# Encoder layer with expert routing: the second merge pass, the last token tile and the first expert body rearranged

## The reference, cut to what matters

```python
h  = rms_norm(x) * (1 + sc1) + sh1
qa, ka, va, qb, kb, vb, ga, gb = split(h @ w_in)
oa, ob = attention(...) @ w_branch_a, window_attention(...) @ w_branch_b
merged = sigmoid(ga) * oa + sigmoid(gb) * ob
x  = x + gt1 * (merged @ w_out)
h2 = rms_norm(x) * (1 + sc2) + sh2
aff = softmax(h2 @ w_router)            # each group routed by itself
g, idx = top_k(aff.T, cap)              # 128 (sample) or 32 (prompt) rows per expert
hid = silu(h2[idx] @ w_e_gate) * (h2[idx] @ w_e_up)
x  = x + gt2 * scatter_add(idx, (hid @ w_e_down) * g)
y  = rms_norm(x)
```

## Time and profile before

| | us |
|---|---|
| median of 3 runs | 2537.7 (2537.65 to 2543.83) |
| the profiled execution, its device time | 2540.18 |
| its span in the trace | 2538.4 |
| PE busy | 2341.3 (92%) |
| DVE busy | 1673.3 (66%) |
| ACT busy | 1214.5 (48%) |
| POOL busy | 1145.7 (45%) |

### The profile page before, as it was taken

The page is one execution under the profiler, slowest core; times in us unless marked ns, Lnnn a source line. Parts: engine busy times, 40 slices in busy tenths (PEclk is TensorE's granted clock), DMA queues, the critical chain, the costliest instruction groups (busy, mean ns, idle before and its releaser), DMA issues.

```text
span 2538.4 us, 54391 instructions
## 1 busy us (share of the span) xinstructions
PE 2341.3 (92%) x23617; PEld 1698.3 (67%) x23724; DVE 1673.3 (66%) x2040; ACT 1214.5 (48%) x1520; POOL 1145.7 (45%) x713
## 2 busy tenths in 40 slices
PE   8599899998999998587899999999999999999993
PEld 3244577655444456456788888888888888888871
DVE  1855466556222466474888878887788878888862
ACT  2322555466111234143655565666555555666552
POOL 0300111122333323254666766785677666776640
PEclk9799899999999999797999999999999999999997
DMA  8010300311212255154989999999999999999965
GB/s 321 14 34 1 117 1 2 133 68 30 80 50 50 81 160 158 50 188 166 325 302 333 325 323 317 328 322 338 319 317 330 336 314 314 341 327 323 318 230 188
DMA packets 255461, 524.86 MB, mean 207 GB/s; under 512 B 8587, under 2 KB 60924, under 8 KB 255100
## 3 DMA queue, kind: packets, MB, share of 16 engines
q1 hardware_dynamic: 244668, 489.95, 55.3%
q0 software_dynamic: 10560, 31.46, 4.4%
HBM read 493.08 MB, written 28.31 MB: 205 GB/s over the span
## 4 chain that ended last, share of the span: by engine, by line
PE 82%; DVE 10%; ACT 3%; DMA 2%; issue 2%; SPq 1%; POOL 0%; DVEq 0%; ACTq 0%; POOLq 0%
PE ps L1579 22%; PE ps L1580 21%; PE ps L1578 21%; PE ps L1920 4%; PE ps L1730 4%; PE ps L1718 4%; PE ps L1699 2%; DVE arena L1181 2%; DVE arena L1373 1%; DVE arena L1251 1%; PE ps L1709 1%; ACT arena L1032 1%; DMA arena<-w_ada 1%; PE ps L1612 1%; DMA arena<-w_e_up 1%
## 5 line engine op out<-in xcount | busy, mean ns | idle before, releaser
L1579 PE MATMUL ps<-arena 128*128 128x160 bf16 (+2 forms) x5556 | 1394.8, 269 | 28.1 <-POOL arena L751 13.6
L1580 PE MATMUL ps<-arena 128*128 128x160 bf16 (+2 forms) x5555 | 1393.9, 269 | 0.2
L1578 PE MATMUL ps<-arena 128*128 128x160 bf16 (+2 forms) x5462 | 1360.0, 267 | 17.4 <-DVE arena L1510 7.7
L1474 DVE TENSOR_TENSOR arena<-arena 128x2048 bf16<-128x2048 f32 x376 | 922.5, 2458 | 185.6 <-ACT arena L895 185.0
L895 ACT ACTIVATE arena<-arena 128x2048 bf16<-128x2048 f32 x384 | 727.1, 1905 | 230.8 <-PE ps L1580 177.6
L1578 PEld LDWEIGHTS ps<-arena 128*128 128x128 bf16 x5560 | 547.5, 98 | 196.5 <-issue 41.9
L1580 PEld LDWEIGHTS ps<-arena 128*128 128x128 bf16 x5560 | 547.4, 98 | 155.6 <-issue 3.3
L1579 PEld LDWEIGHTS ps<-arena 128*128 128x128 bf16 x5560 | 547.4, 98 | 145.3 <-issue 3.0
L820 POOL TENSOR_TENSOR arena<-arena 128x320 bf16<-128x320 f32 x128 | 285.7, 2232 | 10.0
L817 POOL TENSOR_TENSOR arena<-arena,ones 128x320 bf16<-128x320 f32 x128 | 178.3, 1393 | 175.2 <-DVE arena L1510 174.9
L1118 ACT ACTIVATE arena<-ps 128x160 f32<-128x160 f32 x256 | 77.8, 304 | 321.6 <-PE ps L1580 321.5
(11 more groups left out here) (221 smaller groups left out, 2321.5 us busy)
## 6 DMA issues: line engine op xcount, KB each, us to landing
arena<-w_e_gate SPq DMA_DIRECT2D x64, 2048.0 KB, 9.0
arena<-w_e_up SPq DMA_DIRECT2D x64, 2048.0 KB, 9.4
arena<-w_e_down SPq DMA_DIRECT2D x64, 2048.0 KB, 8.1
arena<-w_ada SPq DMA_DIRECT2D x12, 2048.0 KB, 8.6
arena<-w_in SPq DMA_DIRECT2D x32, 512.0 KB, 5.3
arena<-x_sample SPq DMA_DIRECT2D x16, 512.0 KB, 3.5
arena<-w_in SPq DMA_DIRECT2D x3, 2048.0 KB, 16.3
arena<-w_branch_a SPq DMA_DIRECT2D x32, 128.0 KB, 4.3
```

Source lines behind the costliest of these rows:

```text
L1474: ve.tensor_tensor(lo, stage_half(kind, a), hi, ALU.subtract).then_inc(lo_done, 1)
L1578: pe.matmul(out, w_hi, x_hi, start=start, stop=False)
L1579: pe.matmul(out, w_hi, x_lo, start=False, stop=False)
L1580: return pe.matmul(out, w_lo, x_hi, start=False, stop=stop)
```

## The change

In the second pass `GT` is cut in two: a new step `GD` n is DVE's writing of the diagonals, and `GT` n keeps the product and the copy. `GD` n stands one half block ahead of `GT` n. Block order is rotated by one: `second(k)` maps block k of the second pass to output block k - 1 (mod 8), so that its block 0 is block 7 and uses the split weights that `WS` 7 left behind. `WS` 8 and its load are gone; `WS` 9 moves from after `XO` 3 to after `XO` 2. `RT` and `AT` of the last sample tiles move back by a half block, and one of the top-k rounds moves from block 1 to block 6.

The last token tile's `XO` works in two halves of 512 columns, the first after two of the four `OL` pieces; the square root's table is loaded ahead of it. ACT does half of this tile's `X2`. In all `RT`, ACT instead of DVE scales the softmax. `XS` moves behind the last `X2`, and POOL's split of its result behind the last tile's DMAs.

In the first body the split of weight halves becomes one a step: halves 8 to 15 at f = 0 to 7, and halves 0 to 7 of expert 1 at f = 8 to 15. Its fourth quarter takes the places of its first. At the end, the last `down` waits for a quarter's hidden values at a time.

```diff
@@ -183,7 +183,8 @@
-            s += [("GT", n) for n in range(2)]
+            for n in range(2):
+                s += [("GD", n), ("GT", n)]
@@ -191,11 +192,12 @@
-        if p in (1, 3):
-            s.append(("WS", KD + p // 2))
+        if p == 2:
+            s.append(("WS", KD + 1))
-    tail = {(0, 1): [("X2", ns - 1), ("RT", ns - 2), ("AT", ns - 3)], (1, 0): [("RT", ns - 1), ("AT", ns - 2)],
-            (1, 1): [("AT", ns - 1)], (2, 0): [("GT", 2)], (2, 1): [("GT", 3)], (3, 0): [("GT", 4)], (3, 1): [("GT", 5)], (4, 0): [("GT", 6)], (4, 1): [("GT", 7)]}
+    tail = {(0, 1): [("X2", ns - 1)], (1, 0): [("RT", ns - 2), ("AT", ns - 3)], (1, 1): [("RT", ns - 1), ("AT", ns - 2)],
+            (2, 0): [("AT", ns - 1), ("GD", 2)], (2, 1): [("GT", 2), ("GD", 3)], (3, 0): [("GT", 3), ("GD", 4)],
+            (3, 1): [("GT", 4), ("GD", 5)], (4, 0): [("GT", 5), ("GD", 6)], (4, 1): [("GT", 6), ("GD", 7)], (5, 0): [("GT", 7)]}
@@ -203,13 +205,14 @@
-        for _ in range((0, 1, 2, 3, 3, 3, 2, 2)[m]):
+        for _ in range((0, 0, 2, 3, 3, 3, 3, 2)[m]):
-    s += [("FH", 0), ("FH", 1), ("FL", 0), ("O", ns), ("KM",), ("IS",), ("FH", 2), ("FH", 3), ("FL", 1), ("FL", 2), ("XO", ns), ("FL", 3), ("OL", 0), ("OL", 1), ("X2", ns),
-          ("OL", 2), ("RT", ns), ("OL", 3), ("XS",), ("XO", ns + 1), ("AT", ns), ("FH", 4), ("FH", 5), ("X2", ns + 1),
-          ("RT", ns + 1), ("AT", ns + 1), ("FL", 4), ("FH", 6), ("FH", 7), ("FL", 5), ("K", 0), ("I",)]
+    s += [("FH", 0), ("FH", 1), ("FL", 0), ("O", ns), ("KM",), ("IS",), ("FH", 2), ("FH", 3), ("FL", 1), ("FL", 2), ("XO", ns),
+          ("FL", 3), ("OL", 0), ("OL", 1), ("X2", ns), ("OL", 2), ("RT", ns), ("OL", 3), ("AT", ns), ("XO", ns + 1),
+          ("X2", ns + 1), ("XS",), ("FH", 4), ("RT", ns + 1), ("AT", ns + 1), ("FL", 4), ("FH", 5), ("FH", 6), ("FH", 7),
+          ("FL", 5), ("K", 0), ("I",)]
@@ -332,7 +335,7 @@
-        split = [(3 + n) * CH for n in range(6)]
+        split = [(3 + n) * CH for n in (4, 2, 0, 1, 5, 3)]
@@ -460,11 +464,15 @@
-            return ((5, 3), (4, 2), (0, 1), (3, 4))[q][kind]
+            return ((4, 5), (0, 1), (2, 3), (4, 5))[q][kind]
+        def second(k):
+            return (k - 1) % KD
@@ -480,11 +488,7 @@
-                if s < 4:
-                    return []
-                if s < 12:
-                    return [(0, s + 4)]
-                return [(2, 2 * (s - 12)), (2, 2 * (s - 12) + 1)]
+                return [(0, s + AHEAD) if s < AHEAD else (2, s - AHEAD)]
@@ -633,23 +637,22 @@
-            mw_load(KD)
+            mw_load(KD + 2)
-                if p in (1, 5):
-                    k = p // 4
-                    sp.wait_ge(ws_done, 2 * KD + k + 1)
-                    sp.wait_ge(ws_rest, k + 1)
-                    mw_load(KD + k + 2)
+                if p == 4:
+                    sp.wait_ge(ws_done, 2 * KD + 1)
+                    sp.wait_ge(ws_rest, 1)
+                    mw_load(KD + 3)
-                sp.wait_ge(ws_done, 2 * KD + k - 1)
-                sp.wait_ge(ws_rest, k - 1)
+                sp.wait_ge(ws_done, 2 * KD + k - 2)
+                sp.wait_ge(ws_rest, k - 2)
-            sp.wait_ge(ws_done, 3 * KD)
-            sp.wait_ge(ws_rest, KD)
+            sp.wait_ge(ws_done, 3 * KD - 1)
+            sp.wait_ge(ws_rest, KD - 1)
@@ -756,14 +759,15 @@
-                    gp.tensor_tensor(dst[:, s[1], a:a + w], tmp, ones[:, 0:1].to_broadcast([P, w]), ALU.mult).then_inc(mhigh, 1)
+                    m = s[1] if k == "M" else second(s[1])
+                    gp.tensor_tensor(dst[:, m, a:a + w], tmp, ones[:, 0:1].to_broadcast([P, w]), ALU.mult).then_inc(mhigh, 1)
-                    gp.tensor_tensor(dst[:, KD + s[1], a:a + w], tmp, dst[:, s[1], a:a + w], ALU.subtract)\
+                    gp.tensor_tensor(dst[:, KD + m, a:a + w], tmp, dst[:, m, a:a + w], ALU.subtract)\
-                    gp.wait_ge(ws_hi, 2 * m + 1)
+                    gp.wait_ge(ws_hi, 2 * m - 1)
@@ -784,7 +788,7 @@
-                if k == "XS":
+                if k == "XO" and s[1] == NT - 1:
@@ -1084,24 +1088,45 @@
-                    ac.wait_ge(x1_ready, t + 1)
+                    if t < NT - 1:
+                        ac.wait_ge(x1_ready, t + 1)
-                    ac.activation(xn2[:, t % 2], x1[:, t % 2], ACT.Square, accum_out=rs[:, t % 2, 0:1]).then_inc(ssq, 1)
+                    if t < NT - 1:
+                        ac.activation(xn2[:, t % 2], x1[:, t % 2], ACT.Square, accum_out=rs[:, t % 2, 0:1]).then_inc(ssq, 1)
+                    else:
+                        ac.activation(spare[:, 3:4], ones[:, 0:1], ACT.Sqrt)
+                        for h in range(2):
+                            z = slice(512 * h, 512 * h + 512)
+                            ac.wait_ge(x1_half, h + 1)
+                            ac.activation(xn2[:, t % 2, z], x1[:, t % 2, z], ACT.Square, accum_out=rs[:, t % 2, 4 * h:4 * h + 1])\
+                                .then_inc(ssq, 1)
+                if k == "X2" and s[1] == NT - 1:
+                    b, free = job(s, 1)
+                    for q in range(4):
+                        ins = ac.activation(h2T[1][:, 4 + q, :], b[:, q * P:(q + 1) * P], ACT.Identity,
+                                            scale=A2[:, 4 + q, 0:1], bias=modT[:, 28 + q, 0:1])
+                    ins.then_inc(free, 1)
+                    ac.wait_ge(rt_rec, t + 1)
+                    ac.activation(af[:, t % 2], lg[:, t % 2], ACT.Copy, scale=rst[:, t % 2, 2:3]).then_inc(aff_ready, 1)
+                            if h == AHEAD:
+                                for b in range(2):
+                                    ac.wait_ge(x1_out[b], 8 * NT)
+                                    ac.wait_ge(xn2_out[b], 8 * NT)
@@ -1172,9 +1197,9 @@
-            def modulate(s, dst, A, sh, g):
-                for half in range(2):
+            def modulate(s, dst, A, sh, g, halves=(0, 1)):
+                for half in halves:
@@ -1379,10 +1404,10 @@
-                if k == "GT":
+                if k == "GD":
-                    if n % 4 >= 2:
+                    if n >= 2:
@@ -1408,26 +1433,37 @@
-                    ve.wait_ge(out_done, t + 1)
+                    if t < NT - 1:
+                        ve.wait_ge(out_done, t + 1)
-                    o = ps[:, 2 * (t % 2):2 * (t % 2) + 2].rearrange("p a b -> p (a b)")
-                    ve.tensor_tensor(x1[:, t % 2], o, gt1b[g], ALU.mult).then_inc(out_free, 1)
-                    ve.wait_ge(out_free, t + 1)
-                    ve.tensor_tensor(x1[:, t % 2], x1[:, t % 2], xo[:, t % 2], ALU.add).then_inc(x1_ready, 1)
-                    norm_in(NT + t)
+                    if t < NT - 1:
+                        o = ps[:, 2 * (t % 2):2 * (t % 2) + 2].rearrange("p a b -> p (a b)")
+                        ve.tensor_tensor(x1[:, t % 2], o, gt1b[g], ALU.mult).then_inc(out_free, 1)
+                        ve.wait_ge(out_free, t + 1)
+                        ve.tensor_tensor(x1[:, t % 2], x1[:, t % 2], xo[:, t % 2], ALU.add).then_inc(x1_ready, 1)
+                        norm_in(NT + t)
+                    else:
+                        for h in range(2):
+                            z = slice(512 * h, 512 * h + 512)
+                            ve.wait_ge(*((half_done, 1), (out_done, NT))[h])
+                            ve.tensor_tensor(x1[:, t % 2, z], ps[:, 2 * (t % 2) + h], gt1b[g][:, z], ALU.mult).then_inc(last_mul, 1)
+                            ve.wait_ge(last_mul, h + 1)
+                            ve.tensor_tensor(x1[:, t % 2, z], x1[:, t % 2, z], xo[:, t % 2, z], ALU.add).then_inc(x1_half, 1)
+                        ve.wait_ge(ssq, 2 * NT + 1)
+                        link(ve.tensor_tensor(rs[:, t % 2, 0:1], rs[:, t % 2, 0:1], rs[:, t % 2, 4:5], ALU.add))
+                        norm_in(NT + t)
-                    modulate(s, lambda kk: h2T[t % 2][:, kk, :], A2, 24, group_of(tile_at(t)))
+                    modulate(s, lambda kk: h2T[t % 2][:, kk, :], A2, 24, group_of(tile_at(t)), (0,) if t == NT - 1 else (0, 1))
-                    link(ve.reciprocal(rst[:, t % 2, 2:3], rst[:, t % 2, 1:2]))
-                    ve.tensor_scalar(af[:, t % 2], lg[:, t % 2], rst[:, t % 2, 2:3], None, ALU.mult).then_inc(aff_ready, 1)
+                    ve.reciprocal(rst[:, t % 2, 2:3], rst[:, t % 2, 1:2]).then_inc(rt_rec, 1)
@@ -1784,8 +1820,9 @@
-                        pe.wait_ge(ws_done, 2 * KD + m + 1)
-                        pe.wait_ge(ws_rest, m + 1)
+                        if m:
+                            pe.wait_ge(ws_done, 2 * KD + m)
+                            pe.wait_ge(ws_rest, m)
@@ -1816,15 +1853,16 @@
-                    for k0, k1 in ((0, KD - 1), (KD - 1, KD)):
-                        if p == NT - PT_TILES and k1 == KD:
+                    order = list(range(KD)) if p < NT - PT_TILES else [second(n) for n in range(KD)]
+                    for part in (order[:-1], order[-1:]):
+                        if p == NT - PT_TILES and len(part) == 1:
```

(10 more changed lines are left out.)

9 lines of the change are left out of this document (5 added, 4 removed).

## The result

| | us |
|---|---|
| before, median (4 runs) | 2537.7 (2536.8 to 2543.8) |
| after, median (4 runs) | 2503.9 (2502.6 to 2504.5) |
| after / before | 0.9861, 95% interval 0.9844 to 0.9878 |
| profiled execution: before, after | 2540.18, 2503.61 (spans 2538.4, 2501.8) |
| forecast | 2503.7 (2493 to 2519) |

What follows compares the result with a forecast made beforehand. PE was taken as the bound from 1233.73 us on, and ahead of that its waits, mostly for the diagonals. Terms −1.7 − 25.1 − 0.9 − 6.3 = −34.0 turn the median 2537.7 into 2503.7 us, range 2493 to 2519.

Steps and rivals of the forecast that it cites:

- Projection stage: Before the second pass: PE's 1.73 us wait before an `X2`, for DVE's scaling, should go: −1.7 us (0 to −1.8).
- Second pass: Up to `IS`: waits 18.9 instead of 37.7 us, cold matmuls 6.4 instead of 12.7: −25.1 us (−30 to −20).
- The walk along both lists: Second pass: PE's and DVE's work followed from before block 0, giving remaining waits of 18.9 us.
- the third per us waited: Second pass: cold matmuls cost 0.34 us for each us waited, so 6.4 instead of 12.7 us.
- `IS` to the first body: Stage of 51.53 us: last `X2` at 23.3 instead of 25.9, most given back: −0.9 us (0 to −3).
- First body: Body of 68.36 us: one split a step ends DVE's late products, next body starts at 62.1: −6.3 us (−10 to 0).
- The turn of 15.7 us: First body, slowest buffer: load 9.04, high part 1.91, two low parts of 2.46 us, some 15.7 in all.
- End: Last down product: the 5.04 us wait stays, since PE stands until DVE empties expert 14's products: 0.
- A: Second pass: DVE's low parts run unhindered by POOL's, 1.22 instead of 4.25 us: −12 more, 2492; A or like gain 0.12.
- B: First body turns on the loads: three turns cost 7 us more each, 21 in all: 2525; chance 0.15.
- C: Second pass: DVE keeps its backlog, long waits shrink only 2 or 3 us each, some −20: 2509; chance 0.08.
- D: Second pass: PE stays cold at 1.2 GHz from block 2 on: +44.3 us, 2548 in all; chance 0.04.

Runs made afterwards that it cites:

- e3: The changed kernel with the first body's weight halves split as before (8 to 15 at f = 4 to 11, then two per f): 2512.6 us.
- e5: The changed kernel with the gate load issued just ahead of the prompt's gather held until that gather has landed: 2502.6 us.
- f1: The changed kernel with `XS` and the last high and low parts back in their old places, the last tile still in halves: 2499.5 us.
- e9: The changed kernel with the last down product waiting for all hidden values at once, as before: 2505.6 us (one run).
- e2: The kernel before with only the diagonals (`GD`) written a half block ahead: 2511.4 us, ratio 0.9901.
- e4: The changed kernel with POOL's low part of each second-pass block waiting until DVE has written its own: 2492.0 us.
- e1: The changed kernel with the diagonals `GD` n written again directly ahead of `GT` n's product: 2536.2 us, ratio to the kernel before 0.9999.
- e6: The changed kernel with the split of the next weights (`WS`) ahead of `GT` and `GD` of the same half block, on all engines: 2506.8 us.

## Why the prediction was right, and where it wasn't

The time, 2503.9 after 2503.7, is nearer than its steps. From profile to profile the gain was 36.6, not 34.0; the profiled execution of before lay 2.5 above its median and that of after 0.3 below, so the medians moved by 33.8. Against the forecast the steps below are off by +0.6, −2.4, +3.2, −2.3 and −2.4, and the stretch ahead of them was 0.9 longer. That they come to some 2.5 us only, and that the medians took even this back, is luck; that most of the gain lies in the second pass isn't.

- *Projection stage*, −1.7: it was −1.1. The wait of 1.73 went, but one of 0.91 came at an earlier `X2`, behind the place where `WS` 9 now stands.
- *Second pass*, −25.1: −27.5. The walk along both lists named the waits: 4.4 at the last router step (4.7), 0.5, 4.6 and 6.2 for the diagonals (0.2, 4.5, 6.5), none at the others. That the last agrees to 0.3 is partly luck: in e3, e5, f1 and e9, whose second pass is the same program, it was 4.9, and the pass took 108.4 all the same, with more of it in cold matmuls (PE busy 93.06 in e3, 91.84 here). Of the wait at `IS`, 3.0, only 0.7 came: PE ended its `O` 0.8 us later and DVE its joining a good 1 us earlier than in the walk.

  The cold matmuls cost what the forecast gave them, PE was busy 6.3 us less, but the third per us waited isn't a constant: 6.4 us stood beside 16.6 of waits here (0.38), and by the same 85.5 us of warm work e2 has 7.8 beside 15.8 and e4 3.9 beside 8.4, nearly half. So the price came out because the waits were 2.3 shorter than forecast. The walk's own end doesn't fit its sum: `IS` at 1087.7 is 109.8 after the old start of the pass and 111.5 after one 1.7 earlier, while the terms give 110.8.

  The walk gave one total for all edits. I hadn't asked which of them makes it, and where I had to say (e1), I gave the diagonals 10 to 16 of 27.
- *`IS` to the first body*, −0.9: **+2.3**. This step failed. The last `X2` came even earlier than I said (21.2 after `IS` instead of 23.3), and the last affinities at 31.7 instead of 34.3. What I had taken for a matter of POOL's order (the load lands "about at the body's start") was the load's own effect: the gather of 32 rows was issued 1.8 us earlier than before and took 4.1 longer, behind a load of 2048 KB issued just ahead of it. I had both times, the load's and the gather's, and didn't set them side by side.
- *First body*, −6.3: −8.6. The turn of 15.7 us was right in kind: ACT takes up every second load at 11.7, 27.7 and 42.5 us into the body (1151.53, 1167.52, 1182.33), where the sum had 13.0, 28.8 and 44.3. The first was 1.3 shorter, with 7.7 from issue to use instead of 9.04. The same program of this body took 60.7 to 62.1 in e1, e4, e6 and e9, nearer to the 62.1 that I had forecast; up to 2 of the 8.6 may be this one profile's.
- *The second body*: left out, −2.4 (−0.8 in e9). A wait's price is paid behind it, and where the wait ends a stage that part falls into the next.
- *End*, 0: right, as e9 shows.

The failed step (3.2 too hopeful) was covered by the missing one and by the second pass (2.4 more gain each) and the first body (2.3).

**The rivals.** A didn't come by itself; its mechanism is real, as e4 shows, and worth the 12 us that it was priced at (10.5 in the pass, 1.1 ahead of it), but only when POOL is made to wait. B: loads did set the pace of the first body, one in 15 to 16 us on each buffer's turn, but the landings came no later than assumed. C sized the long waits as I sized e1, by 2 to 3 us less; they lost 4.0 to 5.1. D: PE did return to full speed, the granted clock was 0.92 over the pass.

## What to carry to other kernels

Where an engine waits for a small operand that another one makes late, move the making one unit of work ahead before anything else: it gains that unit's whole length at every wait that is longer. Look for pairs of DVE and POOL instructions that begin together on the same data; if the short one goes first, it keeps its own time, and the long one loses at most that much (5.08 us for 4.07 in e6). Here the short one was what PE waited for. And for each small transfer that something waits for, ask what large one was issued just ahead of it, because an edit elsewhere may move the large one there.
